# A seventh place for weight parts and other orders at the seams of a two-block transformer layer

## The chip, the cores and the metric

One core of one Trainium2 chip. The metric is the device time of one execution in microseconds (us). Before the change three runs gave 1146.44, 1147.78 and 1154.98; the median is 1147.78.

## What is computed

Two transformer blocks run one after the other on the same 256 tokens of width 1024, all in float32. Cut to what matters here:

```
first_block:   x = x + 0.5 * ffn(norm(x))                        # 1024 -> 2816 -> 1024, silu(gate) * up
               h = norm(x) @ w_in                                # all projections of the mixer
               x = x + (sig(ga) * (attn @ w_proj_a) + sig(gb) * (mlstm @ w_proj_b)) @ w_out
               x = x + 0.5 * ffn(norm(x))
second_block:  x = x + 0.5 * norm(ffn(norm(x)))                  # norms before and after each branch
               x = x + norm([attn | pool](norm(x) @ w_in_2) @ w_out_2)
               x = x + norm(cross_attention(norm(x), norm(mem)) @ xa_wo_2)
               x = x + 0.5 * norm(ffn(norm(x)))
```

`norm` is an RMS norm over the row. The first mixer has index-picked attention and an mLSTM; the second has ALiBi attention and a causal pooling mixer; the cross attention reads 256 memory rows through `xa_wkv_2`.

## The kernel before

**Split precision.** Every large product is made of three float32r matmuls: high part times high part, low times high, high times low. Activations (`h_hi`, `h_lo`, `f_hi`, `f_lo`, `mem_hi`, `mem_lo`) and weights (`w_hi`, `w_lo`) are both split so.

**Units.** All weights are streamed in 375 units of 512 KB (128 partitions x 1024 columns), listed by `Plan` (L212 on) in the order in which TensorE uses them. For each unit: SyncE loads it into one of six `stage` buffers (`load`, L368), once the low part of the unit six earlier is made; ScalarE copies it to `w_hi` (`hi_to`, L938), once TensorE has used the unit six earlier (semaphore `used`); VectorE subtracts to get `w_lo` (`lo_to`, L1300); TensorE multiplies (`unit`, L414). Parts live in six places, `u % STAGES`. A unit in form "rows" has the activations as stationary operand and 512 weight columns moving, once for each of the two row tiles of 128 tokens: 6 matmuls for each row tile. In form "cols" the weights are stationary and 256 tokens move: 24 matmuls. Four pairs of PSUM banks (`pair[0..3]`) hold the sums; the dictionary `free` says which semaphore gives a pair free.

**Order.** Nothing is scheduled at run time: each engine's program is one hand-written sequence (`tensor_program`, `scalar_program`, `vector_program`, `gpsimd_program`, `sync_program`), and conversions are placed in it by calls such as `hi_to(E + 4)`, "convert up to this unit". The units of each engine are thus in one order, but how many stand between two other instructions is written out.

**Stages.** They are: feed-forward 0 (units 0 to 65), first mixer (`plan.M1` = 66), feed-forward 1 (121), feed-forward 2 (187), second mixer (`plan.M2` = 253), cross attention (`plan.XA` = 285), feed-forward 3 (309). A feed-forward has six blocks of gate and up columns (the first as "rows", the other five as "cols") and a down projection.

**Seams.** Between two stages lies a norm, and it needs whole rows. So the last six units of a stage run first with row tile 0 alone and then with row tile 1 (`tail`, L466, and the loops of six in the mixers). While TensorE is at row tile 1, the other engines finish row tile 0: VectorE adds to `x` (`add`, or `post_part` with its own norm), ScalarE squares (`square`), VectorE makes the mean square, GpSimd the power -0.5 (`root`, L1856, and `post_root`), VectorE scales the rows (`normed`), TensorE transposes (`norm_turn`, L443), ScalarE and VectorE make `h_hi` and `h_lo` (`norm_hi`, `norm_lo`). The next stage then starts likewise with `head` (L454): `n` units with row tile 0, the transposes of row tile 1 after unit `at`, and the same units with row tile 1. A unit counts as used only when row tile 1 is done, so during a tail all six places are held. `n` is 6 with `at` 4 in the feed-forwards, and 4 with `at` 3 in the mixers; cross attention starts with four whole memory units and transposes behind them. The calls at the seams are in `add_tail`, `post_tail`, `add_ffn_tail`, `residual_half` and the mixers' own ends.

**Cross attention** (`cross`): four units for the left half of the values, four and four for the queries, four for the right half of the values, then eight for the output projection. Between them stand `scores`, `turn_heads` and `weigh` for two groups of two heads. `weigh(0)` gives the output of the first group; ScalarE and VectorE split it (`weighed`, semaphore `xolo`), and the output projection's first units need it.

## Time and profile before

| | us |
|---|---|
| median of 3 runs | 1147.78 |
| lowest, highest | 1146.44, 1154.98 |
| profiled execution | 1154.67 |
| its span, first to last instruction | 1152.8 |
| TensorE busy | 1126.1 |
| VectorE, ScalarE, GpSimd busy | 706.5, 557.8, 66.2 |

The profile is of one execution, which was not the median one. For each instruction there is a start, a modelled end, and, where an engine stood idle before it, what ended the idle time. Matmuls overlap in the pipeline, so "busy" lengths of matmuls are longer than their distances from start to start. In the profile's rows the core's mean granted TensorE clock was 0.995 of full speed. Loads of weights averaged 181 GB/s over the span.

### The profile page before, as it was taken

The page shows a single profiled execution, that of the slowest core. Times are in us where ns is not written, and L with a number is a line of the kernel's source. Part 1 is how long each engine was busy: PE and PEld are TensorE (multiplying, and loading weights), DVE is VectorE, ACT ScalarE, POOL GpSimd, SP SyncE. Part 2 cuts the span into 40 slices and gives each one's busy share as a digit, 9 for nine tenths or more (in the row PEclk, how much of TensorE's full clock was granted, in tenths as well). Part 3 has the DMA queues.
Part 4 walks back from the last instruction along what each step waited for, and adds up shares of the span by engine and source line. Part 5 has one row for each costly group of instructions (what it writes and reads, how often), then busy time and mean ns, then how long its engine had stood idle before and what let it go on. Part 6 is the DMA issues. An engine that isn't in the chain of part 4 may idle for free.

```text
span 1152.8 us, 17729 instructions
## 1 busy us (share of the span) xinstructions
PE 1126.1 (98%) x7528; PEld 1019.5 (88%) x7528; DVE 706.5 (61%) x793; ACT 557.8 (48%) x724; POOL 66.2 (6%) x72
## 2 busy tenths in 40 slices
PE   8999999999999999999999999999999998999998
PEld 5999988888989799998889998879978987999986
DVE  5656644778967665564476765465938536665643
ACT  4544444467654444444444544345736536444441
POOL 1000000300000000000020000020411002000000
PEclk9999999999999999999999999999999999999999
DMA  8766655644465576555486566648335535756550
GB/s 281 219 201 199 186 184 149 207 151 128 127 185 156 175 223 195 181 186 201 129 304 195 176 216 188 193 148 304 132 110 202 181 92 161 223 168 202 182 180 36
DMA packets 112338, 209.19 MB, mean 181 GB/s; under 512 B 8690, under 2 KB 18050, under 8 KB 112131
## 3 DMA queue, kind: packets, MB, share of 16 engines
q1 hardware_dynamic: 109714, 198.60, 54.7%
q0 software_dynamic: 2544, 9.45, 2.6%
q8 instruction: 59, 0.97, 0.3%
q14 instruction: 21, 0.16, 0.0%
HBM read 206.98 MB, written 1.05 MB: 180 GB/s over the span
## 4 chain that ended last, share of the span: by engine, by line
PE 86%; DVE 6%; POOL 3%; ACT 2%; issue 2%; DMA 1%; DVEq 0%; POOLq 0%; SPq 0%; ACTq 0%
PE pair L408 85%; DVE w_lo L1304 3%; PE pair L412 2%; DVE xr L1333 1%; DVE h_lo L1341 1%; POOL stat L1858 1%; ACT w_hi L944 1%; ACT xr L950 0%; DMA stage<-in_w_proj_a 0%; POOL xr L1937 0%; POOL xr L1939 0%; ACT h_hi L964 0%; DMA stage<-in_xa_wq 0%; POOL y L1931 0%; POOL win L1931 0%
## 5 line engine op out<-in xcount | busy, mean ns | idle before, releaser
L1304 DVE TENSOR_TENSOR w_lo<-stage,w_hi 128x1024 fp32r<-128x1024 f32 (+1 forms) x375 | 458.2, 1237 | 243.5 <-ACT w_hi L944 241.2
L944 ACT CAST w_hi<-stage 128x1024 fp32r<-128x1024 f32 (+1 forms) x375 | 387.2, 1047 | 310.5 <-PE pair L408 302.0
L408 PE MATMUL pair<-h_hi,w_hi 128*128 128x256 f32 x1504 | 422.6, 281 | 1.3 <-DVE h_lo L1341 1.1
L408 PE MATMUL pair<-h_hi,w_lo 128*128 128x256 f32 x1504 | 419.6, 279 | 0.0
L408 PE MATMUL pair<-h_lo,w_hi 128*128 128x256 f32 x1504 | 419.6, 279 | 0.0
L408 PEld LDWEIGHTS pair<-h_hi,w_hi 128*128 128x128 f32 x1504 | 285.7, 190 | 5.9 <-issue 2.9
L408 PEld LDWEIGHTS pair<-h_hi,w_lo 128*128 128x128 f32 x1504 | 283.6, 189 | 0.0
L408 PEld LDWEIGHTS pair<-h_lo,w_hi 128*128 128x128 f32 x1504 | 283.1, 188 | 0.3
L408 PE MATMUL pair<-w_hi,f_hi 128*128 128x512 f32 x352 | 137.2, 390 | 0.0
L408 PE MATMUL pair<-w_hi,f_lo 128*128 128x512 f32 x352 | 137.0, 389 | 0.0
L408 PE MATMUL pair<-w_lo,f_hi 128*128 128x512 f32 x352 | 137.0, 389 | 0.0
L408 PE MATMUL pair<-w_hi,h_hi 128*128 128x512 f32 (+1 forms) x304 | 120.5, 397 | 10.9 <-DVE w_lo L1304 8.4
L408 PE MATMUL pair<-w_lo,h_hi 128*128 128x512 f32 (+1 forms) x304 | 118.6, 390 | 0.0
L408 PE MATMUL pair<-w_hi,h_lo 128*128 128x512 f32 (+1 forms) x304 | 117.9, 388 | 0.0
L408 PEld LDWEIGHTS pair<-w_hi,h_hi 128*128 128x128 f32 x304 | 57.3, 188 | 26.5 <-issue 8.8
L408 PEld LDWEIGHTS pair<-w_lo,f_hi 128*128 128x128 f32 x352 | 66.1, 188 | 13.8
L408 PEld LDWEIGHTS pair<-w_hi,f_hi 128*128 128x128 f32 x352 | 66.1, 188 | 13.5
L408 PEld LDWEIGHTS pair<-w_hi,f_lo 128*128 128x128 f32 x352 | 66.1, 188 | 13.5
L408 PEld LDWEIGHTS pair<-w_lo,h_hi 128*128 128x128 f32 x304 | 57.3, 189 | 12.2
L408 PEld LDWEIGHTS pair<-w_hi,h_lo 128*128 128x128 f32 x304 | 57.3, 188 | 11.2
L994 ACT CAST f_hi<-act_buf 128x1024 fp32r<-128x1024 f32 (+1 forms) x20 | 19.3, 964 | 59.2 <-DVE act_buf L1365 59.2
L1356 DVE TENSOR_TENSOR act_buf<-act_buf,pair 128x1024 f32<-128x1024 f32 (+1 forms) x24 | 27.2, 1131 | 31.5 <-ACT act_buf L985 31.3
(261 smaller groups left out, 880.4 us busy)
## 6 DMA issues: line engine op xcount, KB each, us to landing
stage<-in_ffn_w_gate SPq DMA_DIRECT2D x88, 512.0 KB, 4.5
stage<-in_ffn_w_up SPq DMA_DIRECT2D x88, 512.0 KB, 4.4
stage<-in_ffn_w_down SPq DMA_DIRECT2D x88, 512.0 KB, 4.3
stage<-in_w_in SPq DMA_DIRECT2D x52, 512.0 KB, 4.2
stage<-in_w_out SPq DMA_DIRECT2D x16, 512.0 KB, 3.6
stage<-in_xa_wkv SPq DMA_DIRECT2D x16, 512.0 KB, 4.5
stage<-in_xa_wq SPq DMA_DIRECT2D x8, 512.0 KB, 4.0
stage<-in_xa_wo SPq DMA_DIRECT2D x8, 512.0 KB, 4.0
```

Of the source, the lines that this page charges most:

```text
L408: return e.matmul(o, l, r, start=start, stop=stop, skip_group_check=True)
L412: return e.transpose(o, i_, m.ident[0:n, 0:n])
L944: e.copy(m.w_hi[u % STAGES][:, 0:w], m.stage[u % STAGES][:, 0:w]).then_inc(s.hi, 1)
L994: e.copy(flat(m.f_hi[n][:, 4 * b:4 * b + w // S, :]), m.act_buf[n][b % 2][:, 0:w]).then_inc(s.fhi, 1)
L1304: e.tensor_tensor(m.w_lo[slot][:, 0:w], m.stage[slot][:, 0:w], m.w_hi[slot][:, 0:w].bitcast(F32), ALU.subtract).then_inc(s.lo, 1)
L1333: e.scalar_tensor_tensor(m.xr[:, t, cols], src[:, t, cols], r, rows[:, cols], ALU.mult, ALU.mult).then_inc(s.xr, 1)
L1341: e.tensor_tensor(lo[:, ks, ts], src, hi[:, ks, ts].bitcast(F32), ALU.subtract).then_inc(s.nlo, 1)
L1356: e.tensor_tensor(buf, buf, m.pair[gate][:, 0:w], ALU.mult).then_inc(s.silu, 1)
L1858: e.tensor_tensor(m.stat[:, t, 3:4], m.stat[:, t, 2:3], m.half_pow[:, 0:1], ALU.pow).then_inc(s.rt, 1)
```

## The change

The parts get a seventh place (`PLACES`), the stages stay six. Every call of `hi_to` and `lo_to` goes one unit further (`AHEAD`), but for the first two of each. The feed-forwards begin with seven units for row tile 0 and transpose after the sixth; the first mixer with five, transposing after the fourth; the second mixer puts one whole memory unit between the row tiles; cross attention puts the first unit of the right value columns behind its transposes and moves the second query half to pair 2 and the right values to pair 1. At the seams one conversion moves from behind the mean square to before it, in `post_part` to between the product and the update of `x`, and on ScalarE ahead of or behind the squares. To make room, `mv` and `xpad` share memory with `ya_hi` and `ya_lo`, and feed-forward 2 keeps `act_buf` in `xk`. The core of the diff:

```diff
+PLACES = 7
+AHEAD = PLACES - 6
...
-        self.w_hi = [sb(f"w_hi{i}", [P, UNIT], F32R, W_REST) for i in range(STAGES)]
-        self.w_lo = [sb(f"w_lo{i}", [P, UNIT], F32R, W_REST) for i in range(STAGES)]
+        self.w_hi = [sb(f"w_hi{i}", [P, UNIT], F32R, W_REST) for i in range(PLACES)]
+        self.w_lo = [sb(f"w_lo{i}", [P, UNIT], F32R, W_REST) for i in range(PLACES)]
...
         whole(wkv, DC, 1024, 512, "rows", *mem, 2)
+        v1 = Block("rows", 512, 0, DC, *mem, 1)
+        add(v1, wkv, 1536, 0, 2)
         whole(d["xa_wq_2"], DC, 0, 512, "cols", *h, 3)
-        whole(d["xa_wq_2"], DC, 512, 512, "cols", *h, 1)
-        whole(wkv, DC, 1536, 512, "rows", *mem, 2)
+        whole(d["xa_wq_2"], DC, 512, 512, "cols", *h, 2)
+        for k in (2, 4, 6):
+            add(v1, wkv, 1536, k, k + 2)
...
-    def head(u, n, i, at, pair):
+    def head(u, n, i, at, pair, between=None):
         for t in range(T):
             for j in range(n):
...
                 if t == 0 and j == at:
                     norm_turn(i, 1, pair)
+            if t == 0 and between is not None:
+                unit(between)
...
     def ffn(n, i, gate, up, t1, turned, d0, d1, nxt, late=0, memory=False):
-        head(F, 6, i, 4, t1)
-        unit(F + 6)
+        head(F, 7, i, 5, t1)
         unit(F + 7)
...
     def mixer1():
-        head(U, 4, 1, 3, 2)
+        head(U, 5, 1, 3, 2)
         free[1] = (s.ev, 1)
-        units(4, 7)
+        units(5, 7)
...
     def mixer2():
-        units(0, 2)
-        head(U + 2, 4, 5, 3, 2)
+        units(0, 1)
+        head(U + 2, 4, 5, 3, 2, U + 1)
...
     def cross():
         units(0, 4)
         norm_turn(6, 1, 0)
         free[2] = (s.ev, 18)
+        units(4, 5)
...
-        units(9, 12)
-        free[1] = (s.ev, 20)
-        units(12, 13)
+        units(10, 13)
+        free[2] = (s.ev, 20)
+        units(13, 14)
         e.wait_ge(s.ev, 20)
         scores(1, 3)
-        units(13, 14)
+        units(14, 15)
         turn_heads(0, 0)
-        units(14, 15)
-        weigh(0, 1)
         units(15, 16)
-        free[2] = (s.ev, 21)
+        free[1] = (s.ev, 21)
+        weigh(0, 2)
         turn_heads(1, 0)
         e.wait_ge(s.xolo, 1)
         units(16, 17)
...
-    def hi_to(n):
+    def hi_to(n, ahead=AHEAD):
+        n += ahead
         for u in range(done[0], min(n, plan.n)):
-            if u >= STAGES:
-                e.wait_ge(s.used, u - STAGES + 1)
+            if u >= PLACES:
+                e.wait_ge(s.used, u - PLACES + 1)
...
# scalar_program, add_ffn_tail
         norm_hi(i, 0, 0)
+        hi_to(E + 5)
+        residual_half(stage, i, 1, 1)
         hi_to(E + 6)
-        residual_half(stage, i, 1, 1)
# scalar_program, post_tail
         if order_by_row:
-            hi_to(E + 4)
             post_square(stage, 1, 0)
         hi_to(E + 4)
         post_square(stage, 1, 1)
-        hi_to(E + 5)
+        hi_to(E + 6)
         residual_half(stage, i, 1, 0)
-        hi_to(E + 6)
         residual_half(stage, i, 1, 1)
...
-    def lo_to(n):
+    def lo_to(n, ahead=AHEAD):
+        n += ahead
# vector_program, post_part
         e.tensor_tensor(m.y[:, t, cols], src, m.gpost[:, cols], ALU.mult).then_inc(s.py, 1)
         if half == 0:
             return
+        lo_to(then)
# vector_program, add_tail
         add(stage, 1, 1, pairs[1], 1.0 if halves else 0.5)
+        lo_to(E + 5)
         mean_square(i, 1)
-        lo_to(E + 5)
         normed(i, 1, m.x)
# vector_program, post_tail
-        post_part(p, stage, 1, 1, pairs[1])
+        post_part(p, stage, 1, 1, pairs[1], E + 5)
         mean_square(i, 1)
-        lo_to(E + 5)
         normed(i, 1, m.x)
```

## Rows read from the trace of the kernel before

**Rows 1.** The page: busy time of each engine, and the high parts' group.

```profile
PE 1126.1 (98%) x7528; PEld 1019.5 (88%) x7528; DVE 706.5 (61%) x793; ACT 557.8 (48%) x724; POOL 66.2 (6%) x72
...
L944 ACT CAST w_hi<-stage 128x1024 fp32r<-128x1024 f32 (+1 forms) x375 | 387.2, 1047 | 310.5 <-PE pair L408 302.0
```

**Rows 2.** The list of waits of TensorE: total us, times, longest.

```profile
PE pair L408 <- DVE w_lo L1304: 8.6, 9, 2.8
...
PE pair L408 <- POOL xr L1939: 1.9, 1, 1.9
```

**Rows 3.** The chain, start and length: the longest piece of two feed-forwards.

```profile
47.24 146.91 PE pair L408 x1044
...
421.27 150.46 PE pair L408 x1044
```

**Rows 4.** The timeline of all engines at the seam into the first mixer.

```profile
201.40 0.16 DVE L1321 SCALAR_TENSOR_TENSOR stat<-stat 128x1 f32<-128x1 f32 x1 [0.81 <-ACT xr L950]
201.48 1.20 DVE L1304 TENSOR_TENSOR w_lo<-stage,w_hi 128x1008 fp32r<-128x1008 f32 x1
...
201.64 1.45 POOL L1858 TENSOR_TENSOR stat<-stat,half_pow 128x1 f32<-128x1 f32 x1 [10.54 <-DVE stat L1321]
...
203.12 1.41 DVE L1333 SCALAR_TENSOR_TENSOR xr<-x,stat,pre_gain 128x512 f32<-128x512 f32 x2 [0.44 <-POOL stat L1858]
204.02 1.23 PE L412 MATMUL pair<-ident,xr 128*128 128x128 f32 x8 [0.72 <-DVE xr L1333]
...
206.31 0.50 PE L408 MATMUL pair<-w_hi,h_hi 128*128 128x512 f32 x1 [1.06 <-DVE h_lo L1341]
```

**Rows 5.** Busy time and granted clock (PEclk) in three stretches.

```profile
core 0: us, PE busy (x) PEld busy (x) DVE busy (x) ACT busy (x) POOL busy (x), PEclk, DMA share, GB/s
197.64:203.13 5.49, 5.49 (x25) 4.32 (x23) 4.24 (x8) 2.54 (x4) 1.45 (x1) 1.00 0.78 243
...
839.00:844.00 5.00, 4.54 (x18) 3.65 (x20) 1.74 (x2) 1.23 (x4) 0.31 (x1) 0.66 0.38 123
960.00:970.00 10.00, 7.15 (x29) 5.67 (x28) 6.57 (x12) 2.87 (x6) 2.54 (x3) 0.83 0.69 226
```

**Rows 6.** GpSimd's timeline: a root with VectorE at rest.

```profile
952.00 0.55 POOL L1858 TENSOR_TENSOR stat<-stat,half_pow 128x1 f32<-128x1 f32 x1 [2.62 <-DVE stat L1321]
```

**Rows 7.** The timeline at the other seams: TensorE after waits, VectorE's norm rows.

```profile
393.93 0.47 PE L408 MATMUL pair<-w_hi,h_hi 128*128 128x512 f32 x1 [0.93 <-DVE w_lo L1304]
...
396.83 0.50 PE L408 MATMUL pair<-w_hi,h_hi 128*128 128x512 f32 x1 [0.39 <-DVE w_lo L1304]
...
583.33 0.51 PE L408 MATMUL pair<-w_hi,h_hi 128*128 128x512 f32 x1 [0.23 <-DVE w_lo L1304]
...
770.50 0.47 PE L408 MATMUL pair<-w_hi,h_hi 128*128 128x512 f32 x1 [0.54 <-DVE w_lo L1304]
...
770.80 1.41 DVE L1333 SCALAR_TENSOR_TENSOR xr<-x,stat,pre_gain 128x512 f32<-128x512 f32 x2 [0.44 <-POOL stat L1858]
...
773.40 0.51 PE L408 MATMUL pair<-w_hi,h_hi 128*128 128x512 f32 x1 [1.28 <-DVE w_lo L1304]
...
776.91 0.50 PE L408 MATMUL pair<-w_hi,h_hi 128*128 128x512 f32 x1 [0.96 <-DVE h_lo L1341]
...
884.49 0.39 PE L408 MATMUL pair<-h_hi,w_hi 128*128 128x256 f32 x1 [1.08 <-DVE h_lo L1341]
...
965.88 0.47 PE L408 MATMUL pair<-w_hi,h_hi 128*128 128x512 f32 x1 [2.85 <-DVE w_lo L1304]
966.17 1.41 DVE L1333 SCALAR_TENSOR_TENSOR xr<-x,stat,pre_gain 128x512 f32<-128x512 f32 x2 [0.44 <-POOL stat L1858]
...
971.21 0.39 PE L408 MATMUL pair<-w_hi,h_hi 128*128 128x512 f32 x1
```

**Rows 8.** The timeline in cross attention, TensorE and VectorE, behind weigh(0).

```profile
926.07 0.58 PE L408 MATMUL pair<-w_hi,mem_hi 128*128 128x512 f32 x1
...
927.51 1.22 DVE L1767 TENSOR_TENSOR h_lo<-pair,h_hi 128x1024 fp32r<-128x1024 f32 x1 [4.43 <-ACT h_hi L1241]
...
929.03 1.04 PE L412 MATMUL pair<-ident,pr 128*128 128x128 f32 x8
...
930.35 0.47 PE L408 MATMUL pair<-w_hi,h_hi 128*128 128x512 f32 x1 [0.29 <-issue]
```

More of the change, by code:

```diff
@@ L145, in __init__, with ffn_tiles @@
         self.f_hi, self.f_lo, self.act_buf = [], [], []
-        def ffn_tiles(n, sb):
+        def ffn_tiles(n, sb, buf=None):
             self.f_hi.append(sb(f"f_hi{n}", [P, FC, S], F32R, F_REST))
             self.f_lo.append(sb(f"f_lo{n}", [P, FC, S], F32R, F_REST))
-            self.act_buf.append([sb(f"act_buf{n}_{i}", [P, 1024]) for i in range(2)])
+            self.act_buf.append([sb(f"act_buf{n}_{i}", [P, 1024]) for i in range(2)] if buf is None else buf)
         ffn_tiles(0, sb.branch())
         mix = sb.branch()
-        self.ya_hi, self.ya_lo = mix("ya_hi", [P, 4, S], F32R, H_REST), mix("ya_lo", [P, 4, S], F32R, H_REST)
+        over = mix.branch()
+        self.mv = mix("mv", [P, T, 512], F32, H_REST)
+        self.xpad = mix("xpad", [P, 4, S + 3], F32, H_REST)
+        self.ya_hi, self.ya_lo = over("ya_hi", [P, 4, S], F32R, H_REST), over("ya_lo", [P, 4, S], F32R, H_REST)
         self.yb_hi, self.yb_lo = mix("yb_hi", [P, 4, S], F32R, H_REST), mix("yb_lo", [P, 4, S], F32R, H_REST)
-        self.xpad = mix("xpad", [P, 4, S + 3])
-        self.mv, self.mo = mix("mv", [P, T, 512]), mix("mo", [P, T, 512])
+        self.mo = mix("mo", [P, T, 512])
         self.kvn = mix("kvn", [P, T, 336])
@@ L185, in __init__ @@
         self.mem_hi, self.mem_lo = memory("mem_hi", [P, DC, S], F32R, H_REST), memory("mem_lo", [P, DC, S], F32R, H_REST)
-        ffn_tiles(2, memory.branch())
+        xk = flat(self.xk[:])
+        ffn_tiles(2, memory.branch(), [xk[:, 0:1024], xk[:, 1024:2048]])
         mix = memory.branch()
@@ L839, in cross @@
                 e.wait_ge(s.nlo, part_at(6, 1, j // 2))
-            units(4 + j, 5 + j)
+            units(5 + j, 6 + j)
         free[3] = (s.ev, 19)
-        units(8, 9)
+        units(9, 10)
         def scores(hp, pair):
@@ L936, in scalar_program @@
     done = [0]
-    def hi_to(n):
+    def hi_to(n, ahead=AHEAD):
+        n += ahead
         for u in range(done[0], min(n, plan.n)):
             w = plan.width(u)
-            if u >= STAGES:
-                e.wait_ge(s.used, u - STAGES + 1)
+            if u >= PLACES:
+                e.wait_ge(s.used, u - PLACES + 1)
             e.wait_ge(loads[u % STAGES], plan.load_at[u])
-            e.copy(m.w_hi[u % STAGES][:, 0:w], m.stage[u % STAGES][:, 0:w]).then_inc(s.hi, 1)
+            e.copy(m.w_hi[u % PLACES][:, 0:w], m.stage[u % STAGES][:, 0:w]).then_inc(s.hi, 1)
         done[0] = max(done[0], n)
@@ L1173, in mixer1 @@
         residual_half(1, 2, 1, 0)
+        hi_to(E + 5)
+        residual_half(1, 2, 1, 1)
         hi_to(E + 6)
-        residual_half(1, 2, 1, 1)
     def mixer2():
@@ L1218, in cross @@
         evac(U + 3, 2, m.xv[:, :, 0:512], view=lambda ps: ps[:, :].rearrange("p (t n) -> p t n", t=T))
-        hi_to(U + 13)
-        evac(U + 7, 3, flat(m.xq[:, 0:4, :]))
-        hi_to(U + 15)
+        hi_to(U + 14)
+        evac(U + 8, 3, flat(m.xq[:, 0:4, :]))
+        hi_to(U + 16)
         def exps(hp, pair):
@@ L1243, in cross @@
         exps(0, 0)
-        hi_to(U + 17)
-        evac(U + 11, 1, flat(m.xq[:, 4:8, :]))
+        hi_to(U + 18)
+        evac(U + 12, 2, flat(m.xq[:, 4:8, :]))
         hi_to(U + 19)
@@ L1248, in cross @@
         turned(0, 0)
-        hi_to(U + 20)
-        weighed(0, 1)
         hi_to(U + 21)
-        evac(U + 15, 2, m.xv[:, :, 512:1024], view=lambda ps: ps[:, :].rearrange("p (t n) -> p t n", t=T))
+        weighed(0, 2)
+        evac(U + 15, 1, m.xv[:, :, 512:1024], view=lambda ps: ps[:, :].rearrange("p (t n) -> p t n", t=T))
         turned(1, 0)
@@ L1262, in scalar_program @@
     square(m.x, 0, 1)
-    hi_to(1)
+    hi_to(1, 0)
     norm_hi(0, 0, 0)
-    hi_to(2)
+    hi_to(2, 0)
     e.wait_ge(s.x1, 16)
@@ L1298, in vector_program @@
     done, chained = [0], [0]
-    def lo_to(n):
+    def lo_to(n, ahead=AHEAD):
+        n += ahead
         for u in range(done[0], min(n, plan.n)):
-            w, slot = plan.width(u), u % STAGES
+            w, slot = plan.width(u), u % PLACES
             e.wait_ge(s.hi, u + 1)
-            e.tensor_tensor(m.w_lo[slot][:, 0:w], m.stage[slot][:, 0:w], m.w_hi[slot][:, 0:w].bitcast(F32), ALU.subtract).then_inc(s.lo, 1)
+            e.tensor_tensor(m.w_lo[slot][:, 0:w], m.stage[u % STAGES][:, 0:w], m.w_hi[slot][:, 0:w].bitcast(F32), ALU.subtract).then_inc(s.lo, 1)
         done[0] = max(done[0], n)
@@ L1384, in add, with post_part @@
         e.scalar_tensor_tensor(xt, src, weight, xt, ALU.mult, ALU.add).then_inc(s.xup, 1)
-    def post_part(p, stage, t, half, pair):
+    def post_part(p, stage, t, half, pair, then=0):
         src, cols = m.pair[pair][:, t * 512:(t + 1) * 512], slice(512 * half, 512 * half + 512)
@@ L1744, in cross @@
         norm_lo(6, 1, 0)
-        lo_to(U + 14)
+        lo_to(U + 15)
         def score_max(hp, pair):
@@ L1769, in cross @@
         score_max(0, 0)
-        lo_to(U + 16)
+        lo_to(U + 17)
         probs(0)
@@ L1776, in cross @@
         lo_to(U + 20)
-        weighed(0, 1)
+        weighed(0, 2)
         lo_to(U + 22)
@@ L1788, in vector_program @@
     normed(0, 0, m.x)
-    lo_to(1)
+    lo_to(1, 0)
     norm_lo(0, 0, 0)
-    lo_to(2)
+    lo_to(2, 0)
     e.wait_ge(s.x1, 16)
```

2 lines of the change are left out of this document (1 added, 1 removed).

## The prediction

> **What bounds the kernel now.** I read the page's busy times first: TensorE works 98% of the span [rows 1]. Only its gaps and the length of its matmuls can therefore give time back. Of the two engines that convert the weights, ScalarE's idle time before a high part ends almost always with TensorE giving a buffer free, not with a load [rows 1]. So it is the six places for parts, not the six stages or the memory, that hold the conversions back. The list of waits comes second. TensorE waits 8.6 us in all for low parts of weights, in nine places, and 1.9 us once for GpSimd's pooling [rows 2]. The timeline of TensorE then places them: nearly all lie at the seams, where one stage's last units run row tile by row tile and the next begins the same way [rows 4, 7]. The chain comes last, for the long stretches. The same 1044 matmuls of a feed-forward take 146.91 us in the first and 150.46 us in the second [rows 3]. That is 3.55 us of slower steps with no wait in it.
>
> **How the profiled execution stands to the median.** It took 1154.67 us, 1152.8 of it span, and the median is 1147.78, so 6.9 less. Two feed-forwards in the slow step instead of none would be 7.1. I take this for the difference: the median run has mostly the quick step. The sum below is of waits, and is taken from either time alike.
>
> **The seventh places and AHEAD.** No arithmetic is added. Every call of hi_to and lo_to goes one unit further, every conversion waits for the release of a unit one earlier, and a load waits for a low part that is now one unit earlier too. Inside a stage these shifts cancel: the same number of conversions stands between two other instructions of ScalarE, VectorE and the load queue, and only TensorE has a unit more in hand. At a seam the last six units hold their places until their second row tile. Before, nothing of the next stage can be converted until then; now its first unit is, and VectorE has one conversion (1.2 us) less between the release and the norm's rows.
>
> **Low parts and the root.** At a seam VectorE now makes a low part before the mean square, not between it and the norm. The old one (1.20 us) began before GpSimd's root and the root took 1.45 us [rows 4]; with VectorE at rest it takes 0.55 [rows 6]. VectorE also idles 0.81 us before the last piece of the mean [rows 4], so a low part put there delays it by 0.4. Root at 202.05, norm from 202.65 in place of 203.12: 0.5 earlier. Bounds: nothing if the root stays at 1.45, 0.9 if the delay vanishes.
>
> **Into the first mixer.** Twenty-four matmuls, four half units, take 5.49 us, so a half unit (one row tile) takes 1.37 [rows 5]. TensorE is through with its four at 203.3. It waits 0.72 for the norm's rows, transposes, and waits 1.06 for the second tile's low half [rows 4]. In the new order the first rows come at 203.35 and the second at 204.05; transposing ends at 204.6; then comes the narrow unit's first row tile, nine matmuls of 336 columns, 9 x 0.229 x 336/512 = 1.35 us, to 206.0. By then the second tile is converted. The old second tile began at 206.31 without that piece: gain 0.3 + 1.35 = 1.7. Bound below: 1.2 with the long root.
>
> **Into the second and third feed-forward.** The waits are 0.93 and 0.39, and 0.23 [rows 7]. A matmul that had waited starts its successors some 0.15 later than an unbroken one, which I add to each. Seven half units before the second row tile cover the transposes and the conversion, and by the order above each low part is ready 1 us or more ahead of its unit. Gains 1.7 and 0.4. What is late next is the seventh unit's low part, after the norm: 1.2 us of work that ends within 0.2 of TensorE's need. Into the first feed-forward I put nothing: TensorE waits there for the first loads and the start, which stay.
>
> **Into the second mixer.** The waits are 0.54, 1.28 and 0.96 [rows 7]. The memory's second unit moves from before the head to between the row tiles. The head is therefore reached 24 x 0.114 = 2.74 us sooner and six half units become four and a whole one. Without its waits the old head would end near 772.7, so the new one reaches the transposes near 769.9. The norm began at 770.80 [rows 7]; a low part now stands ahead of the x update (1.2 later), but the high part between the two squares has gone (0.9) and the root is short (0.9), which leaves about 0.4: 770.4. Rows at 771.1 and 771.8, transposes to 772.5, the whole unit to 775.2, against the old 776.91: 1.7. One wait of 1.2 us takes the place of three.
>
> **Into cross attention.** The wait of 1.08 [rows 7] is covered by the unit of the right value columns, now behind the transposes: 1.2. But this unit's block shifts what follows. Before, the block's last unit stood between weigh(0) and the second turn_heads. Low parts of the first heads' output were ready at 927.51 + 1.22 = 928.73, which is 2.66 after 926.07, where TensorE had gone on [rows 8]; the unit hid that. Now the unit stands before weigh(0), and behind it only the transposes, about 0.9, separate it from the wait on xolo. That is a **new wait of 1.8 us**, with unit 16, weigh(1) and the rest of the stage queued behind it; an idle of 0.29 there goes. I take +1.5. Bounds: 0, if something else already stood there, and 1.8.
>
> **Into the last feed-forward.** The wait is 2.85 us [rows 7], and the granted clock right behind it is at half, 1.2 of 2.4 GHz, for part of the stretch (0.83 on average over 10 us [rows 5]). With ahead-made parts the head, begun at 957.5 (four half units before 965.88 - 2.85), passes six without a wait, to 965.7. The norm (966.17 before [rows 7]) comes at 965.6: first rows 966.3, second 967.0, transposes to 967.5, then the seventh unit's low part, made after the norm, at 968.2. Its row tile ends at 969.6. The old second tile began at 971.21 [rows 7] with a half unit less done: 1.6 + 1.4 = 3.0, of which about half is the clock. Bound below 2.4.
>
> **A place where a rule speaks against a piece.** In post_part a low part now comes between the product with the gain and the x update, just where GpSimd's post root runs. In the trace a root that meets a low part ends 0.4 us after it ([rows 4]: 202.68 and 203.09). If that happens at the three seams with a post norm, the x update is 0.4 later each time, 1.2 in all; since the root is issued before the product I count nothing and keep 1.2 for the range. The Trainium skill, SBUF — State Buffer, section "Who interferes with whom", says that VectorE with two SBUF inputs and a reading GpSimd instruction exclude each other, and that the first to issue holds the port; by it the root, issued first, would keep its 0.55, and the low part would start late instead.
>
> **Nothing** for the reordered tiles, the act_buf in xk, and the two long mixer waits (1.9 for the pooling [rows 2], one for attention copies): their chains run through ScalarE, VectorE and GpSimd, whose order relative to TensorE's stays.
>
> **Sum.** 1.7 + 1.7 + 0.4 + 1.7 + 1.2 - 1.5 + 3.0 = 8.2 us. From the profiled execution 1146.5; from the median 1147.78 - 8.2 = **1139.6 us**.
>
> **Rivals.**
> - *The slow step comes more often.* It has no cause that the order of work shows, so it can fall either way. One or two more feed-forwards in it than in the median run: 1143.2 or 1146.7. Chance 0.22.
> - *Waits move.* The clock falls after the new wait (1.7 us for 3.4 us at half: it fell also around the 1.9 us wait at 839, where the mean is 0.66 [rows 5]), the roots stay long at three seams (1.8) and post roots collide (1.2): 1144.3. Chance 0.15.
> - *Slower than before.* The slow step in all four feed-forwards, because transposes now come at another moment of the head: 4 x 3.55 = 14.2, so 1153.8. It decides from 8.2/3.55 = 2.3 feed-forwards more than in the median run. For it: the second has it and the first does not, with the same code. Against: nothing that starts it moves. Chance 0.06.
> - *The change does not do what it says.* The stages stay six, so if loads bound the conversions the seam waits stay and the new one is paid: 1149.3. Against it stands ScalarE's idle time [rows 1]. Chance 0.05.
> - *More than told.* The new wait is hidden (1.5) and a third of the mixers' waits goes (2): 1136 or less. Chance 0.10.
>
> My forecast holds the remaining 0.42. **Range** 1134.5 to 1148.5: down to the last rival, up to two slow feed-forwards and some of the moved waits. What one can tell from no change is about 1%, 11.5 us. Faster by more takes most of the last rival and an edge of the forecast, 0.12; slower by more the worst of the third, 0.03; within 1% is 0.85.
>
> **What would show it.** After: no wait for w_lo above 0.3 at the heads of the second and third feed-forward and of the first mixer; one wait of about 1.2 for xr into the second mixer; two of 0.7 into the last feed-forward; a wait of 1.8 for h_lo behind turn_heads(1); roots of 0.55 where they were 1.45; full clock around the last seam. The forecast is wrong if w_lo still heads the list of waits, if the x1044 pieces differ from the old by more than the waits do, or if new waits for stages' loads appear.

## The result and the profile after

The changed kernel takes **1135.18 us** (median of 9 runs, 1134.09 to 1142.51) against 1147.45 for the kernel before in the same session (9 runs, 1144.11 to 1155.08): ratio 0.9885, 95% interval 0.9864 to 0.9906. That is 12.3 us, where 8.2 were forecast. (The ratio is the record's own estimate over both sets of runs and not the quotient of the two medians, which is 0.989.) The number lies in the predicted range, but the chance of 0.85 for "within 1%" was on the wrong side. Its profiled execution took 1135.18, of it span 1133.4; before it was 1152.8, so the two traces differ by 19.4.

The page of the changed kernel, with the parts that answer to [rows 1]. TensorE works 12.2 us less, and the roots of the pre norms (L1870) have a mean of 554 ns; before they had 895.

```profile
PE 1113.9 (98%) x7528; PEld 1010.3 (89%) x7528; DVE 705.7 (62%) x793; ACT 558.1 (49%) x724; POOL 60.6 (5%) x72
...
L956 ACT CAST w_hi<-stage 128x1024 fp32r<-128x1024 f32 (+1 forms) x375 | 387.1, 1048 | 297.1 <-PE pair L417 285.2
...
L1870 POOL TENSOR_TENSOR stat<-stat,half_pow 128x1 f32<-128x1 f32 x16 | 8.9, 554 | 532.4 <-DVE stat L1333 532.4
```

TensorE's part of the list of waits (total us, times, longest) answers to [rows 2]. The low parts of weights have gone from 8.6 us in nine waits to 2.7 in three; 2.2 us of either sum are two waits at the start of the kernel, which the change doesn't touch, so at the seams 6.2 became 0.5. The 1.9 for the pooling stays, the 1.5 for h_lo is new, and the rows of the norm (xr) are now waited for four times.

```profile
PE pair L417 <- DVE w_lo L1316: 2.7, 3, 1.9
...
PE pair L421 <- ACT iqT L1070: 2.0, 1, 2.0
...
PE pair L417 <- POOL xr L1951: 1.9, 1, 1.9
...
PE pair L421 <- DVE xr L1345: 1.8, 4, 0.9
...
PE pair L417 <- DVE h_lo L1779: 1.5, 1, 1.5
...
PE pair L417 <- ACT iqT L980: 1.3, 1, 1.3
```

The timeline at the seam into the first mixer, all engines, answers to [rows 4]. The last low part ends at 201.12, ahead of the mean's last piece (L1333); the root takes 0.55 in place of 1.45, and TensorE waits 0.20 for the rows in place of 0.72.

```profile
199.92 1.20 DVE L1316 TENSOR_TENSOR w_lo<-stage,w_hi 128x1008 fp32r<-128x1008 f32 x1
...
201.22 0.16 DVE L1333 SCALAR_TENSOR_TENSOR stat<-stat 128x1 f32<-128x1 f32 x1
...
201.45 0.55 POOL L1870 TENSOR_TENSOR stat<-stat,half_pow 128x1 f32<-128x1 f32 x1 [10.88 <-DVE stat L1333]
...
202.94 1.23 PE L421 MATMUL pair<-ident,xr 128*128 128x128 f32 x8 [0.20 <-DVE xr L1345]
```

TensorE's timeline at the other seams, against [rows 7] and [rows 8]: one wait into the second mixer, one in cross attention behind the second turn of heads, and two into the last feed-forward, where 2.85 stood.

```profile
762.41 1.23 PE L421 MATMUL pair<-ident,xr 128*128 128x128 f32 x8 [0.92 <-DVE xr L1345]
...
917.63 0.47 PE L417 MATMUL pair<-w_hi,h_hi 128*128 128x512 f32 x1 [1.53 <-DVE h_lo L1779]
...
953.46 1.23 PE L421 MATMUL pair<-ident,xr 128*128 128x128 f32 x8 [0.39 <-DVE xr L1345]
...
955.16 0.50 PE L417 MATMUL pair<-w_hi,h_hi 128*128 128x512 f32 x1 [0.48 <-DVE w_lo L1316]
```

Windows of the changed kernel: the attention indices of the first mixer, the pooling of the second, the last seam. The granted clock is full around the last two (0.66 and 0.83 before, [rows 5]). In the first it is 0.83 over 20 us, that is 3.4 us twice at 1.2 of 2.4 GHz; the same 20 us of the kernel before have 0.94, with one such stretch that ends 1 us behind the window.

```profile
225.00:245.00 20.00, 18.68 (x127) 17.75 (x126) 12.74 (x24) 9.67 (x12) 2.45 (x2) 0.83 0.58 184
825.00:835.00 10.00, 8.11 (x64) 7.09 (x62) 3.37 (x5) 3.37 (x7) 3.36 (x5) 1.00 0.47 159
950.00:960.00 10.00, 9.13 (x43) 7.03 (x42) 5.63 (x10) 4.02 (x8) 3.85 (x3) 1.00 0.63 199
```

The chain of the changed kernel (start, length) for the second, third and last feed-forward. The first row answers to the 150.46 in [rows 3]; the other two had 92.41 and 145.03 in the chain before.

```profile
418.15 146.93 PE pair L417 x1044
...
659.74 91.17 PE pair L417 x546
...
978.23 141.49 PE pair L417 x1020
```

**Where the 19.4 us are.** I measure a seam as the time from the first matmul of a stage's first unit to that of its unit 8 (7 in the first mixer, 6 in the second), and cross attention's rest from there to the last feed-forward's first unit.

| place | before | after | gain | forecast |
|---|---|---|---|---|
| into the first mixer | 21.68 | 19.84 | 1.84 | 1.7 |
| into the second feed-forward | 24.72 | 22.87 | 1.85 | 1.7 |
| into the third | 23.38 | 22.87 | 0.51 | 0.4 |
| into the second mixer | 21.15 | 18.71 | 2.44 | 1.7 |
| into cross attention | 24.26 | 22.81 | 1.45 | 1.2 |
| rest of cross attention | 61.89 | 63.09 | -1.20 | -1.5 |
| into the last feed-forward | 27.57 | 24.35 | 3.22 | 3.0 |
| sum | | | **10.1** | 8.2 |
| slow step gone, three pieces (3.53, 1.24, 3.54) | | | 8.3 | 0 |
| half clock at the pooling gone (rest of the second mixer 88.69 to 87.05) | | | 1.6 | 0 |
| rest of the first mixer (168.02 to 169.14), start | | | -0.6 | 0 |

The seams' 10.1 us repeat in every trace, as the experiments show. The three rows below the sum don't, but for the 1.24: they tell how these two executions differ.

### The profile page after: what moved, and what is told of

The parts are those of the page before. It is cut to its first block, busy times and chain, and to the rows that moved or that the text cites. A ratio compares the mean times of both kernels' runs of the same rounds, so it can differ in the third digit from the quotient of the medians.

```text
span 1133.4 us, 17728 instructions
## 1 busy us (share of the span) xinstructions
PE 1113.9 (98%) x7528; PEld 1010.3 (89%) x7528; DVE 705.7 (62%) x793; ACT 558.1 (49%) x724; POOL 60.6 (5%) x72
## 4 chain that ended last, share of the span: by engine, by line
PE 90%; DVE 4%; POOL 2%; ACT 2%; issue 2%; DMA 1%; DVEq 0%; POOLq 0%; SPq 0%; ACTq 0%
PE pair L417 88%; PE pair L421 2%; DVE w_lo L1316 2%; DVE xr L1345 1%; POOL xr L1949 0%; POOL xr L1951 0%; DMA stage<-in_w_proj_a 0%; POOL y L1943 0%; POOL win L1943 0%; DVE h_lo L1353 0%; ACT xr L962 0%; DVE x L1416 0%; ACT w_hi L956 0%; POOL stat L1870 0%; ACT h_hi L976 0%
## 5 line engine op out<-in xcount | busy, mean ns | idle before, releaser
L417 PEld LDWEIGHTS pair<-w_hi,f_hi 128*128 128x128 f32 x352 | 66.1, 188 | 13.6
L962 ACT ACTIVATE xr<-x 128x512 f32<-128x512 f32 x28 | 17.7, 631 | 49.3 <-DVE x L1396 33.1
L1870 POOL TENSOR_TENSOR stat<-stat,half_pow 128x1 f32<-128x1 f32 x16 | 8.9, 554 | 532.4 <-DVE stat L1333 532.4
```

The source lines that it names most:

```text
L417: return e.matmul(o, l, r, start=start, stop=stop, skip_group_check=True)
L962: e.activation(m.xr[:, t, cols], src[:, t, cols], ACT.Square, accum_out=m.stat[:, t, half:half + 1]).then_inc(s.sq, 1)
L1870: e.tensor_tensor(m.stat[:, t, 3:4], m.stat[:, t, 2:3], m.half_pow[:, 0:1], ALU.pow).then_inc(s.rt, 1)
```

## Experiments

Twelve kernels ran, each beside the kernel before. The kernel before had medians of 1147.6 to 1149.1 in the sessions; over all its 84 runs the median is 1148.8 and the lowest 1143.0. Seam lengths repeat within 0.05 us from trace to trace (0.2 into the second mixer) unless an experiment's edit or a fall of the clock lies in the seam, so one trace is enough to read them. What varies from trace to trace lies elsewhere: the start of the kernel up to unit 8 took 36.9 to 40.7 us over the 14 traces, the first mixer behind its seam 163.5 to 172.1.

### The kernel before once more

No edit.

> The kernel before, once more, for a second trace. Theory 1 (the slow step): where the distance between two 256-column matmuls is 118 ns and not 113, it is a state that an execution falls into at the transposes of act_buf or a later break, and not a property of a place. Then this trace shows it in other feed-forwards than the first one did (there: the second, the last third of the third, the fourth), and its times fall again on steps of some 3.5 us above 1144. Theory 2: the step belongs to the place (addresses, what runs beside); then the same feed-forwards are slow again and the first is quick.

Measured: 1150.77 (12 runs, 1145.41 to 1158.87), ratio 1.002 [0.9997, 1.0042]. The chain, start and length:

```profile
47.82 146.91 PE pair L408 x1044
...
424.24 146.93 PE pair L408 x1044
...
666.31 92.41 PE pair L408 x546
...
993.88 145.03 PE pair L408 x1020
```

The second feed-forward, 150.46 in [rows 3], now has the quick step, by the same code. So the slow step of a whole feed-forward can come or stay away with the same code, and one trace without it is no gain of the change. The pieces of 92.41 and 145.03 came back, which left open whether those two are.

### The changed kernel once more

No edit.

> The changed kernel once more, nothing edited. Theory (the change takes 10.1 us out of seven seams whatever the execution does, and the rest of a single run is the slow step of the 256-column matmuls and falls of the granted clock, drawn anew): all seam lengths repeat within 0.1 us (into the first mixer 19.84, first feed-forward 22.87, last feed-forward 24.35), the median is 1135 +- 1.5 and its ratio to the kernel before 0.986 to 0.991; the last third of the third feed-forward shows the quick step again (at most 4 slow units, where three traces with the old order of that seam show 14). Rival (the changed order brought the slow step down everywhere, so that the first profile was its rule): again no slow step in the first, second and last feed-forward. Other rival (the low median of the changed kernel was luck of one session): median over 1139, ratio over 0.992.

Measured: 1136.37 (6 runs, 1133.84 to 1139.23), ratio 0.9901 [0.9879, 0.9923]. All seam lengths are those of the table within 0.04. No feed-forward is in the slow step, and 91.17 stands again. Both theory and first rival allow this; three kernels below with the changed orders have a whole feed-forward in the slow step (first and last, second, last), which speaks against that rival. Over both sessions the changed kernel has a median of 1135.2 in 15 runs and a lowest of 1133.8: 1.4 between the two, where the kernel before has 5.8. The 84 runs reach a lower lowest by their number alone; 15 drawn from them at random have 2.3 to 6.3 between median and lowest (nine draws in ten), so the smaller number of runs doesn't explain the 1.4.

### Heads turned early in cross attention

```
         scores(1, 3)
-        units(14, 15)
         turn_heads(0, 0)
+        units(14, 15)
+        weigh(0, 2)
         units(15, 16)
         free[1] = (s.ev, 21)
-        weigh(0, 2)
         turn_heads(1, 0)
```

> The changed kernel with turn_heads(0) right behind scores(1), unit 14 behind it, weigh(0) and then unit 15, so that a unit again covers the split of the first heads' output. Theory: the wait of 1.5 us for h_lo behind turn_heads(1) goes and nothing takes its place: 1.5 us less than the changed kernel, 1133.7 where that has 1135.2. Rival: ScalarE's copies of the turned heads stand behind the second exponentials, so TensorE waits for them before weigh(0) instead: no difference.

Measured: 1134.1 (4 runs, 1131.16 to 1134.86), ratio 0.9864 [0.9842, 0.9886]. The rest of cross attention falls from 63.09 to 61.31 and h_lo of L1779 is gone from TensorE's waits. Three of the waits that are left in the list:

```profile
PE pair L417 <- DVE w_lo L1316: 2.7, 3, 1.9
...
PE pair L417 <- POOL xr L1951: 1.9, 1, 1.9
...
PE pair L417 <- ACT iqT L980: 1.5, 1, 1.5
```

So the new wait was what the prediction named, and it was avoidable: a unit must stand between weigh(0) and the second turn. Total and seam agree (1 to 2 us).

### Six units in the head instead of seven, seven places kept

```
-        head(F, 7, i, 5, t1)
+        head(F, 6, i, 4, t1)
+        unit(F + 6)
```

> The changed kernel, but the feed-forwards begin with six units and transpose after the fifth, as before. Theory: low parts stay ready (no wait for w_lo over 0.3), but the transposes come 1.4 us before the norm's rows: +0.5 us into the second feed-forward, 0 to 0.4 into the third, +1.2 into the fourth, in all +2: 1137. Rival: the seventh unit is only cover that was not needed and the seventh place alone brings the gain: +0.3 at most. The slow step: if it hangs on the place of the transposes of act_buf in time, this kernel's times scatter as those of the kernel before; if not, as those of the changed one.

Measured: 1136.68 (5 runs, 1134.93 to 1138.79), ratio 0.9894 [0.9874, 0.9913]. The total is what I had expected (1137), its parts are not. Into the second and third feed-forward nothing changes (22.87 both), against my 0.5 and 0.4: six half units were enough to cover the norm. What the gain there does come from, the runs with six places tell below. Into the last it costs 2.2 (24.35 to 26.58), a longer wait for the rows and a half clock behind it. TensorE's row, and the window:

```profile
952.71 1.31 PE L421 MATMUL pair<-ident,xr 128*128 128x128 f32 x8 [1.77 <-DVE xr L1346]
```

```profile
950.00:960.00 10.00, 8.23 (x34) 6.32 (x33) 4.78 (x9) 3.41 (x8) 3.85 (x3) 0.83 0.52 167
```

0.39 became 1.77, and 1.00 became 0.83.

### Low part behind the mean, as before

```
-        lo_to(E + 5)
         mean_square(i, 1)
+        lo_to(E + 5)
         normed(i, 1, m.x)
```

and the same in the tail with a post norm, where `lo_to(then)` inside post_part goes.

> The changed kernel with the low part of the sixth unit back between the mean square and the norm at all seams (in post_part nothing is put in). Theory: GpSimd's roots take 1.45 us again instead of 0.55 at five seams. Into the first mixer the norm comes 0.5 later and TensorE waits 0.5 longer. At the three seams with a post norm the x update comes 1.2 earlier, which outweighs the longer root, so the norm comes 0.3 earlier there. In all within 0.5 us of the changed kernel. Rival: the short roots carry a real part of the gain: 2 us slower.

Measured: 1135.91 (6 runs, 1134.72 to 1141.77), ratio 0.989 [0.9867, 0.9913]. The roots are long again and the seam into the first mixer is 0.54 longer (20.38). The others stay within 0.05. The page's row, and the timeline (VectorE and GpSimd) of that seam:

```profile
L1871 POOL TENSOR_TENSOR stat<-stat,half_pow 128x1 f32<-128x1 f32 x16 | 13.4, 839 | 529.6 <-DVE stat L1333 529.6
```

```profile
204.36 1.20 DVE L1316 TENSOR_TENSOR w_lo<-stage,w_hi 128x1008 fp32r<-128x1008 f32 x1
...
204.52 1.45 POOL L1871 TENSOR_TENSOR stat<-stat,half_pow 128x1 f32<-128x1 f32 x1 [10.53 <-DVE stat L1333]
```

The root issued 0.16 behind the low part ends 0.41 after it. The short root is real, but with seven places and the other new orders it is worth 0.5 us at one seam: elsewhere another order of things ends the wait.

### The kernel before with the low part ahead of the mean

In the kernel before, alone:

```
+        lo_to(E + 5)
         mean_square(i, 1)
-        lo_to(E + 5)
         normed(i, 1, m.x)
```

and the same in the tail with a post norm.

> The kernel before with one edit: the low part of the fifth unit after the seam is made ahead of the mean square, not behind it, in add_tail and post_tail. Theory: roots of 0.55 us, and this low part comes up to 1.5 us sooner, which is what TensorE waits for into the second and fourth feed-forward and the second mixer: 4 us less than the kernel before. Rival 1: the low part delays the norm by as much as it comes sooner: no difference. Theory on the slow step: it is drawn anew in each execution, so this kernel too shows it now and then; a kernel whose times never lie on steps of 3.5 would speak against that.

Measured: 1142.74 (7 runs, 1140.67 to 1144.83), ratio 0.9957 [0.9942, 0.9972]. With six places the seams gain 0.54, 0.64, 0.51, 0.90, 0.27 and 1.85, together 4.7. So this part alone is worth almost half of the seams' 10.1, much more than the 0.5 that it is worth on top of the seventh place and the other orders: they overlap. TensorE's waits for low parts fall from 8.6 to 6.4 us, and the roots' mean from 895 to 553 ns; how much of the 4.7 is the earlier low part and how much the short root, this run doesn't separate. The 1.85 at the last seam goes with a full clock there.

### Six places, the changed orders kept

```
-PLACES = 7
+PLACES = 6
```

with the head of six, since seven can't be held.

> The changed kernel with six places and no unit ahead (and so heads of six in the feed-forwards); its orders at the seams, its mixers and its cross attention stay. Theory: what the seventh place gives is the conversion made before the release, 1.2 us of VectorE's work at each seam. Head and first full units, from the first unit of a stage to a fixed later one, take 22.9 us in the second feed-forward and 24.35 in the fourth in the changed kernel; here +1.0 and +2, into the second mixer +1, into cross attention +0.5, into the first mixer +0.3: 5 us in all, 1140. Rival: the orders carry the gain and the place next to none: +1 at most.

Measured: 1146.12 (12 runs, one of them 2885.68, which is no run of this kind, the others 1140.47 to 1151.74), ratio 0.9978 [0.9957, 1.0], where I had expected 1140. TensorE waits 8.5 us for low parts, 3.6 of it at the start of the kernel and 3.85 into the second mixer; there the row and the window are

```profile
771.31 0.80 PE L417 MATMUL pair<-w_hi,h_hi 128*128 128x512 f32 x1 [3.85 <-DVE w_lo L1317]
```

```profile
766.00:776.00 10.00, 6.15 (x22) 4.87 (x22) 4.13 (x8) 1.99 (x6) 3.04 (x6) 0.71 0.78 261
```

A unit between the tiles with only six places starves the second tile: 3.85 of wait and, with the fall of the clock (0.71 in the window), 5.7 us more for the seam (24.41). Of the other seams the second feed-forward's loses 0.6 and the last one's 1.4, and three lose nothing. TensorE's waits into the first mixer and into the second feed-forward (the timeline) are 0.17 and 0.35:

```profile
202.75 1.23 PE L421 MATMUL pair<-ident,xr 128*128 128x128 f32 x8 [0.17 <-DVE xr L1346]
...
397.08 0.50 PE L417 MATMUL pair<-w_hi,h_hi 128*128 128x512 f32 x1 [0.35 <-DVE w_lo L1317]
```

The seams of four kernels side by side show what each part of the change is worth (us, one trace each):

| place | before | before, low part ahead | new orders, six places | changed |
|---|---|---|---|---|
| into the first mixer | 21.68 | 21.14 | 19.81 | 19.84 |
| into the second feed-forward | 24.72 | 24.08 | 23.49 | 22.87 |
| into the third | 23.38 | 22.87 | 22.87 | 22.87 |
| into the second mixer | 21.15 | 20.25 | 24.41 | 18.71 |
| into cross attention | 24.26 | 23.99 | 22.81 | 22.81 |
| rest of cross attention | 61.89 | 61.89 | 63.07 | 63.09 |
| into the last feed-forward | 27.57 | 25.72 | 25.75 | 24.35 |

Without the second mixer the change gains 7.7 us, and 5.7 of them come with six places. The seventh adds 0.6 into the second feed-forward, where the head of seven is worth nothing, and 1.4 into the last. There it helps only through the head of seven: with heads of six TensorE waits 1.77 for the rows with six places and with seven. Only the unit between the row tiles can't do without it, and that unit is worth next to nothing, as the next experiment shows.

### Both memory units ahead of the second mixer's head

```
-        units(0, 1)
-        head(U + 2, 4, 5, 3, 2, U + 1)
+        units(0, 2)
+        head(U + 2, 4, 5, 3, 2)
```

> The changed kernel, but both memory units stand ahead of the second mixer's head again. Theory: TensorE then reaches the transposes 2.7 us later, when the rows are ready, but has nothing to do between them and the second tile's split; a wait of 1.1 to 1.2 for h_lo takes the place of the 0.9 for the rows. So 0.1 to 0.2 us slower, and the 2.4 us gained into the second mixer are the low parts' doing. Rival: the unit between the tiles carries that gain: 1.5 to 2.4 slower.

Measured: the seam is 18.80 in place of 18.71, so the unit between the tiles is worth 0.1, less than the 0.2 by which this seam varies. Against the 20.25 of six places with the low part ahead, the seventh place and the other orders of this seam are worth 1.45; no run parts these two. The total is 1139.88 (6 runs, 1135.38 to 1143.35), 4 above the other versions, which the seam can't explain. Its trace, of the slowest run, has three disturbances outside the edit: a start of 40.7 us (37.5 and 38.4 in the changed kernel), the last feed-forward in the slow step, and half-clock stretches at the start, in the first mixer (two) and at the pooling. I have no cause for these, nor for their coming together in this version.

### The activation buffers' address alone

In the kernel before, the third feed-forward's two act_buf tiles moved into xk, nothing else:

```
-        ffn_tiles(2, memory.branch())
+        xk = flat(self.xk[:])
+        ffn_tiles(2, memory.branch(), [xk[:, 0:1024], xk[:, 1024:2048]])
...
```

`ffn_tiles` takes the two buffers as an argument for this. They stood last in their part of the memory, so no other tile moves.

> The kernel before with one edit: the two activation buffers of the third feed-forward lie in the tile xk, as in the changed kernel, so they and nothing else change their address. All four traces with the old order and the old address show 14 slow units (217 to 230) at the end of that feed-forward, all eight with the changed ones show 2, six of which are other versions of the order, one with six places. Theory A (the address of these buffers decides it): 2 slow units there, and the total 1.3 us under the kernel before. Theory B (the order of the last units and the conversions at this stage's ends decides it, or the place where the part buffers lie): 14 slow units again, total within 1.5 us of the kernel before (1146 to 1149.5). In both the seams keep the lengths of before (first mixer 21.7, first feed-forward 24.7, last 27.6) within 0.2.

Measured: 1146.23 (12 runs, 1142.96 to 1151.62) beside 1149.1 (17 runs), ratio 0.9994 [0.9972, 1.0016], so the total alone tells nothing. The chain does:

```profile
46.76 146.91 PE pair L409 x1044
...
420.30 150.46 PE pair L409 x1044
...
665.92 91.17 PE pair L409 x546
...
990.30 141.49 PE pair L409 x1020
```

The x546 piece is 91.17, as in every kernel with the buffers in xk, and was 92.41 in all three traces with the old address. The seams are those of before. Theory A is borne out, by one trace against three: 1.24 us come from where two buffers lie, an edit that the prediction had put at nothing. How the address acts on TensorE, whose 24 matmuls of a unit then stand 118 instead of 113 ns apart, no run shows; TensorE itself reads only one of the buffers, for eight transposes early in the feed-forward.

### Toward a better version

**Copies first.** With the heads turned early, and ScalarE makes no weight parts between the first two attention copies of the first mixer:

```
-            hi_to(U + min(42 + j, 44))
+            if j > 0:
+                hi_to(U + min(42 + j, 44))
```

> The kernel turn_early, and in the first mixer ScalarE copies the second group's turned probabilities before it converts the next high part, which had waited for a load. Theory: the wait of 2.0 to 2.8 us of TensorE for this copy goes (it hangs on the load of in_w_proj_a by ScalarE's order only): 1.5 to 2.3 us less than turn_early. Rival: the chain of copies and of the evacuation of gb is as long without the load: no difference.

Measured: 1132.1 (6 runs, 1128.71 to 1135.05), ratio 0.9862 [0.984, 0.9885]. TensorE's wait for iqT at L1070 (2.3 in the trace without this edit) is gone.

**Index units earlier.** In addition units 12 and 13 of the first mixer stand ahead of index_scores(0):

```
+        units(12, 13)
         index_scores(0)
...
-        units(12, 13)
```

> The version with heads turned early and without the copies after the first attention copy (1132.1 in its session), and in addition the two units with the index rows' place (12 and 13 of the first mixer) are issued ahead of the index scores instead of behind them. Theory (the wait of 1.3 us at 232.9 us for iqT ends when VectorE and GpSimd have the index rows' copies ready, and the two units, 3.9 us of TensorE, fit in front of it): the wait at L980 goes from 1.3 to at most 0.2, the clock does not fall right behind it, and the median is 1.3 to 3 us under the version without it, 1129 to 1131. Rival (the wait only moves: the units in front of the index scores leave nothing between the scores and the mask that needs them, so that a wait of 1 to 2 us turns up before the attention copies): total within 1 us of 1132. Slower rival (mask work of VectorE comes 3.9 us later and the attention of the first head waits for it): wait of 2 to 4 us at the first head, 1133 to 1136.

Measured: **1128.31** (5 runs, 1127.85 to 1129.1), ratio 0.9831 [0.9809, 0.9853]. First TensorE's row of the version without this edit, then its rows and windows with it:

```profile
235.27 1.91 PE L417 MATMUL pair<-ikT,iqT 64*128 64x128 f32 x16 [1.50 <-ACT iqT L980]
```

```profile
233.94 1.71 PE L417 MATMUL pair<-ikT,iqT 64*128 64x128 f32 x16
235.58 0.28 PE L421 MATMUL pair<-ident,xr 4*128 4x4 f32 x2
235.73 1.97 PE L417 MATMUL pair<-xr,ident 4*128 4x256 f32 x8
```

```profile
225.00:238.00 13.00, 13.00 (x109) 12.24 (x108) 9.28 (x16) 8.92 (x12) 2.33 (x2) 1.00 0.80 248
238.00:241.50 3.50, 3.50 (x20) 3.50 (x19) 3.32 (x8) 0.66 (x1) 0.00 (x0) 0.52 0.36 129
```

The wait is gone and nothing took its place: TensorE is busy for 13.00 of 13 us. Yet the clock halves once right behind, where I had expected no fall, after 3.7 us of matmuls that use 64 and 4 of the array's 128 rows. These matmuls don't decide it either: in the trace with only the heads turned early they stand behind a wait of 1.5, and the clock is full (1.00 over 225 to 245). The first mixer behind its seam went from 165.2 to 163.5, which is the wait. The medians lie 3.8 apart, in two sessions; against the kernel before in each session it is 2.8, and the intervals of the two ratios overlap, so that more than the wait came back isn't shown.

**Pooling later.** In addition the pooling's matmuls of the second mixer stand behind att_turn(1, 3), att_weigh(1, 2) and unit 23, and ScalarE makes the last attention copies ahead of its scaled copies.

> The version with index units ahead of the index scores (1128.3 in its session), and in addition the pooling's matmuls of the second mixer stand behind the last turn of attention rows, one weigh and unit 23, and ScalarE makes the last attention copies ahead of the pooling's scaled copies. Theory (TensorE reaches the pooling at 820.96 and GpSimd has the rows at 822.95; 0.8 + 0.9 + 2.8 us of other work fits in front): the wait of 1.9 us at L1952 goes, the unit behind the last weigh waits 0.5 to 0.8 for the low parts of the pooling, the part of the mixer from its first unit to cross attention is 1.1 to 1.6 shorter, and no clock falls there; median 1126 to 1127.5. Rival (the wait moves whole: the low parts of the pooling end 1.9 us or more behind the last weigh): within 0.5 us of 1128.3. Slower rival (the last weigh waits for the attention copies, which stand behind a conversion on ScalarE): 1129 to 1131.

Measured: **1127.18** (5 runs, 1126.28 to 1131.13), ratio 0.9821 [0.9795, 0.9848]. TensorE's row at the pooling and at the unit behind the last weigh:

```profile
826.07 1.89 PE L417 MATMUL pair<-xr,pw 128*128 128x256 f32 x8
...
829.80 0.50 PE L417 MATMUL pair<-w_hi,h_hi 128*128 128x512 f32 x1 [1.03 <-DVE h_lo L1748]
```

1.9 of wait became 1.03, and the rest of the second mixer 0.9 shorter (87.02 to 86.11), under my 1.1 to 1.6; the remaining wait is longer than my 0.5 to 0.8. It is the lowest median measured, about 8 us under the changed kernel, but its interval overlaps that of the version with the index units earlier.

## Why the prediction was right and wrong

**What held.** The waits at the seams could be had, and their sizes were right: the terms for the first mixer, second and third feed-forward, cross attention and the last feed-forward are within 0.1 to 0.25 of what was measured. The new wait came where it was named, 1.53 for 1.8, with its cost 1.2 for 1.5. Turning the heads early took it away. No wait for loads appeared at the seams. The root took 0.55 where VectorE was at rest. The post roots keep 558 ns (557 before), so the 1.2 us kept for them in the range fell away. The low part there begins as the root ends (757.27, and 756.84 + 0.55, into the second mixer), so the two hardly meet, and no run shows which of them would have had to wait. The two-input low part and a root beside it do exclude each other, as the Trainium skill has it (SBUF — State Buffer, "Who interferes with whom"): 1.45 against 0.55.

**Steps that failed.** The sum was 8.2 and the medians differ by 12.3. Of the 4.1 between them 1.9 are seams (step 1), 1.24 the buffers' address (step 2) and about 1.0 what is left for disturbed stretches (step 3). By these sums the result would have stayed within 1% (11.5) without any one of the three. Step 4 cost no time in the sum but is wrong in its cause.

1. The term of 1.7 for the second mixer. It gained 2.44. Counted from the stage's first matmul, I had the transposes at 9.7 us and their end at 11.1, with the norm at 9.0; the norm began at 8.5 (761.51), the transposes at 9.42 and the whole unit at 10.40 (763.39). The wait was 0.92, not 1.2. With the other six terms each some 0.1 to 0.3 too small, the seam sum is 10.1 instead of 8.2. The unit between the tiles, to which I gave the credit, is worth about 0.1.
2. "Nothing" for "the act_buf in xk". It is worth 1.24 us, all of it in TensorE's step at the end of the third feed-forward.
3. "I take this for the difference: the median run has mostly the quick step." I took one trace's 7.1 us of slow step to be its 6.9 above the median of three. But over 84 runs the kernel before has a median of 1148.8 and a lowest of 1143.0, so its typical run lies 5.8 us above its best, and the traces show slow steps, falls of the clock and a longer start as what such runs carry; the changed kernel's lies 1.4 above. Lowest to lowest the change brings 9.2, less than the 11.3 of seams and address, and median to median over all runs 13.6, more. That the excess over 11.3 is a smaller share of disturbed stretches is a conclusion from this difference; the traces are too few to show it. One such piece follows the edited wait: the half clock in the last seam, behind the wait of 2.85, is in all three traces with the old seam and six places there, and in neither of after. The others come and go: 3.4 us at half clock around the pooling in 2 of 3 traces of before (the one with moved buffers counted) and 1 of 2 of after, two half-clock stretches in the first mixer in one trace of after (169.1 us behind the seam) and none in the other (165.6), whole feed-forwards in the slow step in 4 of 9 and 0 of 6 cases.
4. "So it is the six places for parts, not the six stages or the memory, that hold the conversions back." ScalarE's idle time showed that its conversions wait for places, not that TensorE's seams need a place more. With the new orders and six places the seams into the first mixer, the third feed-forward and cross attention gain all that they gain with seven, and the one into the second feed-forward 1.23 of 1.85. The seventh place has 2.0 of the 7.7 us outside the second mixer, 1.4 of them by the head of seven, and at most part of 1.45 in it. The prediction gave place and order one term at each seam. So its terms for the second and third feed-forward came out right without saying which of the two brings them, and orders alone brought 1.23 and 0.51 of the 1.85 and 0.51.

The rivals "slow step more often" and "waits move" didn't come. That the "change does more than told" (1136 or less, chance 0.10) holds by its number and not by its mechanism: the new wait was not hidden, and the mixers' waits stayed (2.0, 1.3 and 1.9).

**What stays open.** What puts a whole feed-forward in the slow step. It is in 8 of 42 cases over 14 traces (first, second and last feed-forward), never from the start of the third, and lasts to the end of the gate and up units. Four cases are in the 12 of the old seams and four in the 30 of the changed ones, too few to say that the change lowers the share. Nor is it shown why the clock halves behind a wait of 1.3 to 1.9 us in one execution and not in another; it isn't the wait alone, as the version with the index units earlier shows.

## What to carry to other kernels

When a resource is held to the end of a stage, an engine that waits for it doesn't yet show that one place more is worth its refill at each seam: here that gave 0, 0.6 and 1.4 us at three like seams, and 6.6 of the 10.1 us (5.7 outside the second mixer and 0.9 in it) came in kernels with six places, by order alone. Price the edits as alternatives, not as a sum: the order of two VectorE instructions alone had 4.7 of the same 10 us, and 0.5 behind all the others. When a unit is moved to cover one wait, look at what it covered where it stood. And with an execution-to-execution spread, set a trace against the lowest and the median of many runs before saying which of them it stands for.

## What the runs showed of the hardware

- Where two buffers lie that ScalarE and VectorE use decided TensorE's step at the end of a feed-forward: 92.41 us in three traces and 91.17 in the one with them moved, for the same 546 matmuls and with nothing else changed, and 91.17 in all ten traces with the changed address and orders.
- TensorE's clock fell to 1.2 GHz for 3.4 us with no wait ahead of it, behind matmuls on 64 and 4 rows (0.52 granted in 238 to 241.5). Removing the wait there didn't bring the full clock, in either trace that has the edit; the same matmuls with a wait of 1.5 ahead of them passed at full clock in another.
- The 256-column matmuls have two steps, 113 and 118 ns, each held for a whole stretch of a feed-forward: 146.9 and 150.5 us for 1044. The same program shows either.
- A GpSimd root of 0.55 us took 1.45 when it was issued 0.16 us behind a VectorE instruction with two inputs, and 0.55 again with the two in the other order.
